# First norm, block gates, and merged branches of a two-block transformer layer in split fp32: the order of VectorE's work changed

## The reference

```python
# first block (T = 256 tokens x, 256 context tokens ctx)
mx, mc = split(silu(c) @ w_mod + b_mod, 6), split(silu(c_ctx) @ w_mod + b_mod, 6)
hx, hc = modulate(rmsnorm(x, g_norm1), mx[0], mx[1]), modulate(rmsnorm(ctx, g_norm1), mc[0], mc[1])
px, pc = split(hx @ w_in), split(hc @ w_in)          # q, k, v of the attention; q, i, f, b, g of the HGRN
att = latent_attention(...)                           # 8 heads of 64, keys of x and ctx
hg = rmsnorm(o_f + flip(o_b), g_hg) * silu(g)         # bidirectional gated linear recurrence, 4 heads of 128
x = x + mx[2] * (concat(att, hg) @ w_out)             # mx[2]: "gate 1"
x = x + mx[5] * swiglu(modulate(rmsnorm(x, g_norm2), mx[3], mx[4]))   # mx[5]: "gate 2"
x = rmsnorm(x, g_final)
# second block
proj = rmsnorm(x) @ w_in_2                            # q, k, v, two latents, 2 x 1024 gate logits
gates = sigmoid(gate_logits + b_gate)
merged = gates[:D] * (moba(...) @ w_branch_a) + gates[D:] * (mla(...) @ w_branch_b)
x = x + rmsnorm(merged @ w_out_2);  x = x + rmsnorm(relu(rmsnorm(x) @ w_up) ** 2 @ w_down)
```

## Time and profile before

| | us |
|---|---|
| median of 3 runs | 863.47 (862.52 to 864.89) |
| the profiled execution, its own time | 863.47 |
| its span, first to last instruction | 861.7 |
| PE busy (matmuls) | 813.9 (94% of the span) |
| VectorE busy | 423.7 (49%) |
| ACT busy | 420.0 (49%) |
| POOL busy | 402.2 (47%) |
| share of PE in the chain that ended last | 77% |

### The profile page before, as it was taken

The page is one execution under the profiler, slowest core; times in us unless marked ns, Lnnn a source line. Parts: engine busy times, 40 slices in busy tenths (PEclk is TensorE's granted clock), DMA queues, the critical chain, the costliest instruction groups (busy, mean ns, idle before and its releaser), DMA issues.

```text
span 861.7 us, 14284 instructions
## 1 busy us (share of the span) xinstructions
PE 813.9 (94%) x5493; PEld 703.3 (82%) x5493; DVE 423.7 (49%) x659; ACT 420.0 (49%) x645; POOL 402.2 (47%) x184
## 2 busy tenths in 40 slices
PE   5899998989899999999999999999998999999996
PEld 4578875876667899999998888899886899998885
DVE  3547377894464533323425547454354623434335
ACT  4435423534474544443443864655745744444443
POOL 3346000000046455664664897445564466466553
PEclk9899999999999999999999999999999999999999
DMA  9674667216625365566564687353444466655651
GB/s 320 235 271 126 204 230 250 74 49 200 192 80 164 123 202 189 170 195 194 171 188 119 191 212 205 100 147 99 147 148 155 126 194 186 196 178 186 183 158 49
DMA packets 94140, 146.59 MB, mean 170 GB/s; under 512 B 15491, under 2 KB 63856, under 8 KB 94096
## 3 DMA queue, kind: packets, MB, share of 16 engines
q1 hardware_dynamic: 92896, 143.23, 53.7%
q0 software_dynamic: 1168, 2.75, 1.2%
q10 hardware_dynamic: 32, 0.01, 0.0%
HBM read 144.92 MB, written 1.05 MB: 169 GB/s over the span
## 4 chain that ended last, share of the span: by engine, by line
PE 77%; DVE 11%; ACT 4%; issue 3%; POOL 2%; DMA 1%; POOLq 0%; SPq 0%; DVEq 0%; ACTq 0%
PE bank L1763 74%; POOL w_lo L605 2%; ACT w_hi L655 2%; PE bank L2028 1%; DVE hg_queries L1309 1%; DVE w_lo L1150 1%; PE bank L1848 1%; DVE h_f L1213 1%; DVE hg_kf L1302 1%; DVE hg_at L1345 1%; DVE hg_kb L1302 1%; DMA raw<-in_w_in 1%; DMA x<-in_x 1%; PE bank L2330 1%; DVE merged L1682 1%
## 5 line engine op out<-in xcount | busy, mean ns | idle before, releaser
L605 POOL TENSOR_TENSOR w_lo<-raw,w_hi 128x1024 fp32r<-128x1024 f32 (+2 forms) x161 | 391.2, 2447 | 446.5 <-ACT w_hi L655 418.4
L655 ACT ACTIVATE w_hi<-raw 128x1024 fp32r<-128x1024 f32 (+1 forms) x218 | 226.0, 1044 | 214.4 <-PE bank L1763 188.0
L1150 DVE TENSOR_TENSOR w_lo<-raw,w_hi 128x1024 fp32r<-128x1024 f32 x60 | 74.6, 1253 | 143.1 <-ACT w_hi L655 142.9
L1763 PE MATMUL bank<-z_hi,w_hi 128*128 128x256 f32 x384 | 108.9, 284 | 0.0
L1763 PE MATMUL bank<-z_hi,w_lo 128*128 128x256 f32 x384 | 107.3, 279 | 0.0
L1763 PE MATMUL bank<-z_lo,w_hi 128*128 128x256 f32 x384 | 107.2, 279 | 0.0
L1763 PE MATMUL bank<-n_hi,w_hi 128*128 128x256 f32 x352 | 99.6, 283 | 1.4 <-DVE w_lo L1150 0.8
L1763 PE MATMUL bank<-n_lo,w_hi 128*128 128x256 f32 x352 | 99.1, 281 | 0.0
L1763 PE MATMUL bank<-n_hi,w_lo 128*128 128x256 f32 x352 | 99.0, 281 | 0.0
L1763 PE MATMUL bank<-w_hi,mlp_h_hi 128*128 128x512 f32 x216 | 85.5, 396 | 1.4 <-POOL w_lo L605 1.4
L1763 PE MATMUL bank<-w_hi,mlp_h_lo 128*128 128x512 f32 x216 | 85.2, 395 | 0.0
(11 more groups left out here) (404 smaller groups left out, 1577.7 us busy)
## 6 DMA issues: line engine op xcount, KB each, us to landing
raw<-in_w_in SPq DMA_DIRECT2D x54, 512.0 KB, 4.5
raw<-in_w_down SPq DMA_DIRECT2D x54, 512.0 KB, 3.7
raw<-in_w_gu SPq DMA_DIRECT2D x44, 512.0 KB, 3.5
raw<-in_w_mod SPq DMA_DIRECT2D x32, 512.0 KB, 4.3
raw<-in_w_up SPq DMA_DIRECT2D x32, 512.0 KB, 3.7
raw<-in_w_mod SPq DMA_DIRECT2D x32, 256.0 KB, 6.1
raw<-in_w_out SPq DMA_DIRECT2D x12, 512.0 KB, 3.8
raw<-in_w_in SPq DMA_DIRECT2D x8, 336.0 KB, 3.0
```

What stands on the lines that cost most here:

```text
L605: nc.gpsimd.tensor_tensor(wl[:, w % SPL, 0:size], raw[:, slot_raw, 0:size], wh[:, w % SPL, 0:size].bitcast(F32), ALU.subtract).then_inc(s_ ...
L655: nc.scalar.activation(wh[:, w % SPL, 0:size], raw[:, slot_raw, 0:size], ACT.Copy).then_inc(s_hi, 1)
L1150: V.tensor_tensor(wl[:, w % SPL, :], raw[:, slot_raw, :], wh[:, w % SPL, :].bitcast(F32), ALU.subtract).then_inc(s_lod, 1)
L1763: return nc.tensor.matmul(out_, l, r_, start=start, stop=stop, skip_group_check=True)
```

## The change

It reorders work on four engines and changes where some values lie.

1. **Start.** "x diag" and "x rstd" go ahead of the second half of `mod_rows(0)`; `mod_rows(1)` goes from ahead of the ff loop to between k = 0 and k = 1 of its first chunk. ACT makes the high part of chunk 0 ahead of everything else and the small exponential of the lower bounds before k = 2. VectorE makes the low part of chunk 0 (POOL did), between `h 0` and `hl 0`, and finishes `h`, `hl` of k = 0 before those of k = 1; the small instructions on columns (gate bias, gains, lower bounds) come later.
2. **Block gates.** The four broadcasts go to n = 10, 11 (gate 1) and n = 12, 13 (gate 2), all in banks 6 and 7, and the four bias additions into m = 5, 6, 6, 7 of VectorE's loop.
3. **Output projection of the first block.** k = 0 starts before the last value matmuls: its first two banks when "exp 15" is done, its other two when "pT 15" is copied; `values(7)` stands between k = 0 and k = 1, and "cat lo 1" is waited for at k = 2. `hg_out(1..3)` works on PSUM banks 6 and 7 in halves of 512. Chunk 33's low part is VectorE's.
4. **MLP ends.** The low part of the last chunk of either MLP is VectorE's.
5. **Branches.** Sigmoid's function table is loaded before `o_hi(1)`; the high parts of chunks 47 to 49 come in another order; chunk 46's low part is VectorE's. Branch b is multiplied and added in place in its PSUM banks, in four pieces; `merged_b` and the six `keep_clock` matmuls ahead of the output projection are gone.

```diff
         def by_dve(w):
-            return (12 <= w < W_END["g"] or c1 in (2, 3) or ...
-                    or w in (W2["branch a"] - 1, W2["branch b"] - 1) or c2 in (-2, -1) or ...)
+            return (w == 0 or 12 <= w < W_END["g"] or c1 in (2, 3) or ...
+                    or w == W_END["out"] - 1 or w in (W2["branch a"] - 1, W2["branch b"] - 3, W2["branch b"] - 1)
+                    or c1 == 5 + 12 * MLP1_TRIPS or c2 == 3 + 12 * MLP2_TRIPS or c2 in (-2, -1) or ...)
...
 ACT
-            act.wait_ge(DV.sem, DV["lb max"])
-            nc.scalar.activation(stat[:, 40:56], stat[:, 24:40], ACT.Exp)...
             for k in range(KT):
-                if k % 2 == 0:
+                if k == 0:
+                    hi(1)
+                elif k == 2:
+                    act.wait_ge(DV.sem, DV["lb max"])
+                    nc.scalar.activation(stat[:, 40:56], stat[:, 24:40], ACT.Exp)...
+                    hi(3)
+                elif k % 2 == 0:
                     hi(k + 1)
...
+            load_functions(SIGMOID)
             o_hi(1)
             hi2(44)
             for j in range(16):
                 nc.scalar.activation(gates[:, j, :], gates[:, j, :], ACT.Sigmoid, bias=bgc[:, j:j + 1])...
-                if j == 1:
-                    hi2(45)
-                elif j % 4 == 3:
-                    hi2(45 + j // 4)
+                if j in (1, 7, 11):
+                    hi2({1: 45, 7: 46, 11: 49}[j])
             hi2(50)
-            for b, (k0, k1) in enumerate(MERGED):
-                if b in (2, 4):
-                    hi2(51 + b // 2)
+            for b in range(4):
+                if b == 2:
+                    hi2(52)
                 act.wait_ge(DV.sem, DV[f"merged {b}"])
-                nc.scalar.activation(flat(mgh, k0, k1 - k0), flat(mgf, k0, k1 - k0), ACT.Copy)...
+                nc.scalar.activation(flat(mgh, 2 * b, 2), ps[4 + b][:], ACT.Copy)...
...
 VectorE
+            x_diagonals()
+            dve.wait_ge(PE.sem, PE["rows"])
+            done(V.tensor_copy(cols[:], ps[7][:, 0:R_N]), "cols")
             modulation(0)
-            x_diagonals()
             own("xT 1 3")
             dve.wait_ge(AC.sem, AC["x rstd"])
-            h_pair(0)
+            h_product(0)
+            chunk_lo(0, number["w"][0] % RAW)
+            h_low(0)
+            h_product(1)
+            h_low(1)
...
                 elif step == 1:
                     dve.wait_ge(AC.sem, AC["hg rstd"])
                     own("hg gated")
-                    tick(V.tensor_tensor(xn[:, 1, :], flat(gg, 0, 4), xn[:, 0, :], ALU.mult), "hg o")
+                    own("gate 2 b 1")
+                    for j in range(2):
+                        ins = V.tensor_tensor(ps[6 + j][:], flat(gg, 2 * j, 2), xn[:, 0, 512 * j:512 * j + 512], ALU.mult)
+                    tick(ins, "hg o")
...
+                    dve.wait_ge(s_gb, 32)                 # m == 5
+                    gate_bias("gate 1", ga1, 0)
+                elif m == 6:
+                    gate_bias("gate 1", ga1, 1)
+                    gate_bias("gate 2", ga2, 0)
+                elif m == 7:
+                    gate_bias("gate 2", ga2, 1)
                 probs(2 * m + 1)
...
-            cat_lo(1)
-            gate_bias("gate 2", ga2, 0, 1)
+            cat_lo(1)
             for step in range(1, 4):
                 hg_out(step)
+            level_lo(W_END["out"] - 1)
...
+            branch_lo("branch b", 3)
+            branch_lo("branch b", 1)
+            def merged(b):
+                dve.wait_ge(AC.sem, AC[f"gate {8 + 2 * b + 1}"])
...
+                done(V.tensor_tensor(ps[4 + b][:], ps[4 + b][:], flat(gates, 8 + 2 * b, 2), ALU.mult), f"mb {b}")
+                tick(V.tensor_tensor(ps[4 + b][:], ps[4 + b][:], flat(mgf, 2 * b, 2), ALU.add), f"merged {b}")
+            merged(0)
+            for b in range(1, 4):
+                merged(b)
+                merged_lo(b - 1)
+            merged_lo(3)
...
 TensorE
+            pe.wait_ge(DV.sem, DV["x diag"])
+            mm(ps[5][:], ones, dg4[:]..., True).then_inc(PE.sem, PE.tick("x rstd"))
             mod_rows(0, (1,))
             pe.wait_ge(DV.sem, DV["cols"])
             mod_cols(0)
-            pe.wait_ge(DV.sem, DV["x diag"])
-            mm(ps[5][:], ones, dg4[:]..., True).then_inc(PE.sem, PE.tick("x rstd"))
-            mod_rows(1)
...
-                    if kk == 0 and 1 <= j < 3:
+                    if kk == 0 and j < 3:
                         mod_rows(j + 1)
...
-                elif n == 14:
+                elif n in (10, 11):
                     pe.wait_ge(DV.sem, DV["hg gated"])
-                    gate("gate 1", rowb, 0, 6, 0)
-                    gate("gate 1", rowb, 0, 6, 1)
+                    gate("gate 1", rowb, 0, n - 10)
+                elif n in (12, 13):
+                    pe.wait_ge(DV.sem, DV[f"gate 1 b {n - 12}"])
+                    gate("gate 2", rowc, 2, n - 12)
...
             def joined(k):
-                if k == 4:
+                if k == 0:
+                    pe.wait_ge(AC.sem, AC["exp 15"])
+                    pe.wait_ge(DV.sem, DV["cat lo 0"])
+                elif k == 1:
+                    values(7)
+                elif k == 2:
+                    pe.wait_ge(DV.sem, DV["cat lo 1"])
+                elif k == 4:
                     pe.wait_ge(DV.sem, DV["cat lo"])
-            rows_out(next1, joined, ch, cl, "out")
+            rows_out(next1, joined, ch, cl, "out", lambda: pe.wait_ge(AC.sem, AC["pT 15"]))
...
             pe.wait_ge(DV.sem, DV["ma 3"])
-            keep_clock(0, 6)
-            rows_out(next2, lambda k: pe.wait_ge(DV.sem, DV[f"merged lo {max(b for b, ... if k0 <= k)}"]), mgh, mgl, "out 2")
+            rows_out(next2, lambda k: pe.wait_ge(DV.sem, DV[f"merged lo {k // 2}"]), mgh, mgl, "out 2")
```

More of the change, by code:

```diff
@@ L1168, in x_from_psum @@
                                    ps[XT_BANKS[v][pair]][:].rearrange("p (k t) -> p k t", k=2)), f"xT {v} {pair}")
[L1170 to L1184, removed]
+            for v in range(2):
+                for pair in range(4):
+                    x_from_psum(v, pair)
             def x_diagonals():
@@ L1204, in modulation, with h_product @@
                                             op0=ALU.add, op1=ALU.mult), f"modc scale {g}")
+            def h_product(k):
+                if k >= 4:
+                    own(f"hl {k - 4}")
+                for v in range(2):
+                    c = slice(T * v, T * v + T)
+                    ins = V.scalar_tensor_tensor(out=hf[:, k % 4, c], in0=xT(k)[:, c], scalar=modc[:, 8 + k, v:v + 1],
+                                                 in1=rowb[:, c], op0=ALU.mult, op1=ALU.mult)
+                tick(ins, f"h {k}")
@@ L1206, in h_pair, with h_low @@
+            def h_low(k):
+                dve.wait_ge(AC.sem, AC[f"hh {k}"])
+                for v in range(2):
+                    c = slice(T * v, T * v + T)
+                    ins = V.scalar_tensor_tensor(out=hl[:, k, c], in0=hf[:, k % 4, c], scalar=modc[:, k, v:v + 1],
+                                                 in1=hh[:, k, c].bitcast(F32), op0=ALU.add, op1=ALU.subtract)
+                tick(ins, f"hl {k}")
             def h_pair(g):
                 for k in (2 * g, 2 * g + 1):
-                    if k >= 4:
-                        own(f"hl {k - 4}")
@@ L1211, in h_pair @@
[L1211 to L1215, removed]
-                for k in (2 * g, 2 * g + 1):
[L1217 to L1222, removed]
+                    h_product(k)
@@ L1658, in _, with branch_lo @@
             o_lo(1)
-            def branch_lo(name):
-                w = W2[name] - 1
+            def branch_lo(name, back):
+                w = W2[name] - back
                 chunk_lo(w, (N1 + w - N1W) % RAW)
-            branch_lo("branch a")
+            branch_lo("branch a", 1)
             for b in range(4):
@@ L1885, in project, with gate @@
                         after.pop(0)()
-            def gate(name, sums, strip, bank, j):
+            def gate(name, sums, strip, j):
                 s = 32 * (strip + j)
-                mm(ps[bank + j][:], ident[:, s:s + 1].broadcast_to([P, P]), sums[:], True).then_inc(PE.sem, PE.tick(f"{name} {j}"))
+                mm(ps[6 + j][:], ident[:, s:s + 1].broadcast_to([P, P]), sums[:], True).then_inc(PE.sem, PE.tick(f"{name} {j}"))
             def shift_and_scale():
@@ L2111, in _, with rows_out @@
                 probs_t(2 * m + 1)
-            gate("gate 2", rowc, 2, 0, 0)
-            values(7)
-            gate("gate 2", rowc, 2, 0, 1)
-            def rows_out(chunk, made, xh, xl, name):
+            def rows_out(chunk, made, xh, xl, name, made_1=None):
                 slots = []
```

68 lines of the change are left out of this document (35 added, 33 removed).

## The result

| | before | after |
|---|---|---|
| median, us | 864.18 (4 runs, 862.52 to 865.27) | 855.12 (4 runs, 854.82 to 855.46) |
| ratio | | 0.9897, 95% interval 0.9878 to 0.9915 |
| span of the profiled execution | 861.7 | 853.7 |

A forecast was written before the change was run, and what follows sets the result against it. PE, busy for 94% of the span, was taken as the bound. Savings of 4.4 (start), 0.3 (gates, output projection), 1.4 (MLP ends) and 6.2 (branches) sum to 12.3; 863.5 - 12.3 = 851.2, rounded 851, range 847.5 to 857.

The forecast's parts named there:

- 1, start: Start of the kernel, up to the first projection: reordering saves 4.4 us, ends 1.4 and 6.5.
- the 6.7 of earlier stream: At the start: PE's first projection matmul begins at 21.9 instead of 28.59, 6.7 us earlier.
- the 1.9 of `mod_rows(1)`: At the start: mod_rows(1) moves from PE's wait into its stream and costs 1.92 us.
- the 0.35 of clock: At the start: the new stream runs cold from 21.9 to 26, costing 0.35 us more than before.
- rival (a): The start gives a quarter: cold clock lasts, or loads hold PE at mod_rows(2); 854.5 us, chance 0.12.
- three signs: Prediction wrong if PE waits for a DMA before mod_rows(2), the cold clock grows, or gates delay attention by over 2.
- 2 and 3: Block gates and first output projection: saves 0.3 us, ends minus 1.5 and plus 2; PE's wait returns at k = 2.
- 4: MLP ends: PE's idle of 0.72 and 0.66 before the last two chunks goes, saving 1.4 us (0 to 1.4).
- 5: Branches to the end of the second output projection: idle and constants' matmuls go, saving 6.2 us, ends 4.0 and 7.5.

The follow-up runs named there:

- rows1_half: Changed kernel with the first half of mod_rows(1) put back ahead of the projection; 849.92 us, ratio 0.9846.
- the whole: Changed kernel with both halves of mod_rows(1) ahead of the projection; 851.47 us, ratio 0.9848.
- merge_sbuf: Changed kernel with its four 128x512 merges kept in SBUF again; 856.80 us, ratio 0.9915.
- start_only: Kernel before with only the edits of the start; 863.43 us, ratio 0.9986.
- out28_dve: Changed kernel with chunk 28's low part on VectorE and chunk 29's high part ahead of the table load and exponential; 852.47 us, ratio 0.9876.
- pool46: Changed kernel with the low part of chunk 46 back on POOL; 853.97 us, ratio 0.9889.
- clock_back: Changed kernel with the six constants' matmuls back between branch b and the output projection; 855.98 us, ratio 0.9905.
- no_out: Changed kernel with the gates and block one's output projection as before the change; 855.77 us, ratio 0.9899.

## Why the prediction was right in its range and wrong in its first step

**1, start: wrong, by all of its 4.4.** The two parts of the step that were worked out from instructions held. The sequence from the columns to the first projection matmul is 2.95 (20.48 to 23.43; 19.0 to 21.9 was forecast). The first projection matmul starts at 22.12 to 23.52 in the seven kernels with this start, where 21.9 was forecast. In the changed kernel's own profiled execution it is late because c landed late. Its chain from the start of the span (start us, us, what) has

```profile
1.38 4.84 DMA rows_c<-in_c_ctx
```

and from there ACT's sums of squares and root lead to the broadcast at 15.90; in rows1_half PE could take c at 4.46 instead of 6.26, and the broadcast starts at 14.68. Before, the root was ready at 13.47 and needed only at 20.14. The reordering took that slack away; the prediction put the broadcast at about 14.6 without saying what it hangs on.

What failed is the sentence "all loads behind it move up about 2 us ... which I take to be just enough". I had followed SP only to the issue that POOL held, and costed `mod_rows(1)` as 1.92 of matmuls. It also releases four of the six `raw` slots, and moving it behind k = 0 released them later. So the next loads went out 1.7 later (0.4 to 1.9 over the seven kernels), not 2 earlier: 0.99 of waiting at `mod_rows(2)`, and POOL's work slid onto VectorE's column instructions, 1.76 more. Term by term: the 6.7 of earlier stream came out as 5.16, the 1.9 of `mod_rows(1)` as 1.92, the 0.35 of clock as 0.86 with restarts (the cold clock lasted to 28 rather than 26), and 0.99 + 1.76 = 2.75 stood in no term. That gives -0.37 for 4.4.

Two of the three signs that the prediction named for being wrong were there: PE waited for a DMA before `mod_rows(2)`, and the cold clock grew. The range held because rival (a) lay in it, and its 854.5 is nearest to the 855.12. Rival (a) named the place, "the loads that moved up only 2 us hold PE at `mod_rows(2)`", but priced the loss at 3.2 of the 4.4, gave it 0.12, and did not see that the loads would go out later than before. Its argument against, that PE's waits there are for columns and not data, was read off a timeline in which the slots were freed early.

**2 and 3: right.** Forecast 0.3, measured 0.55 and 0.52. The last transposes of probabilities are 0.47 later (forecast 1.1), the wait came back at k = 2 for POOL, 1.55 (forecast about 2), and the one at k = 6 is gone. The wait of 0.60 at k = 1 had no term. Shifted by the 1.13 that the trace was behind, the forecast has k = 2 at 258.8 and k = 3 at 262.2, the rows 258.64 and 262.06.

**4: right.** Neither wait is left; 1.89 for 1.4, the idle and a restart of some 0.25 each.

**5: right.** 6.64 for 6.2: one wait near k = 1 of 0.62 (forecast 0.9), 0.29 at chunk 44 (forecast 0.4), additions of 0.70 beside POOL. By the runs, banks are worth 2.0 of it, chunk 46 1.3, the constants 1.5; the other 1.8, the table load's place in it, was not taken apart. The table load took 1.28 with ACT's next copy at its heels (612.77, then 614.06). The Trainium skill, "ScalarE: Activation LUTs", What ACT_TABLE_LOAD costs, puts a switch at about 2.66 with a drain, by which I had estimated this part at about 5.2. The measurement decides: no row of these kernels shows that drain.

**Between 64 and 189**, where nothing was changed, the changed kernel lost 0.76. The same matmuls took 124.62 at a mean granted clock of 0.97, where before had 0.99 and 123.86, and the kernel with the start alone 1.00:

```profile
64.48:187.17 122.69, 114.55 (x688) 93.52 (x689) 89.87 (x126) 52.74 (x73) 15.78 (x9) 1.00 0.51 165
```

Over the fourteen profiled kernels, in all of which the change leaves this stretch alone, it took 122.69 to 125.26, and the kernel with the start alone, fastest here, was 1.5 slower than the kernel before in the next stretch. So 0.76 is within the scatter of single executions. I had no term for it, and what decides it was not pursued.

## What to carry to other kernels

When a step moves, list what it releases as well as what it costs: a group of matmuls that frees a load's buffer is worth its place in the queue of loads, and moving it back took away here as much as starting the whole stream 5 us earlier gave. If an engine waits for the first result anyway, put into that wait the work whose inputs have landed and whose buffers the next loads need. Whether to stop at what has landed is not settled here: the half gave 0.9846, the whole, with its wait of 1.94 for the load, 0.9848. Follow one period past the edit, to where the other engines' work slides: here the low parts of the next stage came to lie on small instructions that they block.

## What the runs showed of the hardware

**A small instruction can be blocked as long as a large one.** The 128 x 4 instruction with two SBUF inputs took 1.98 while POOL subtracted (1.95 to 2.03 in seven kernels), 0.16 otherwise; the 128 x 8 one just ahead of it, with one input in a bank, took 0.17 beside the same POOL instruction. The blocked one ended at 49.50, POOL's at 49.47. The Trainium skill, "SBUF — State Buffer", SBUF: two separate sides, says that whichever starts first has the port pair for its whole instruction; the rows agree: in merge_sbuf, too, 128 x 512 instructions with two SBUF inputs took 1.56, 2.18 and 2.89 beside POOL, and 0.68 or 0.69 without it.

**The clock after a wait of the same length goes two ways.** After PE's wait of 2.12 before j = 2, the same matmuls up to j = 3 took 11.6 in four kernels (start_only, the changed kernel, out28_dve, pool46) and 13.2 in three (merge_sbuf, clock_back, no_out), where the granted clock was at the lower of its two levels, 1.2 GHz, for a part of them. What decides it stays open.
